# State-space groups: VectorE's two products of decay and scores stand in a row, the fourth modulation tile behind both

## The reference, cut to what matters

```python
mod = (c_act @ w_mod[l] + b_mod[l])[:, None, :]
sh1, sc1, g1, sh2, sc2, g2 = jnp.split(mod, N_MOD, axis=-1)
...
decay = jnp.exp(jnp.where(causal, seg, -jnp.inf))
cb = jnp.einsum('bign,bjgn->bgij', C_c, B_c)
y_intra = jnp.einsum('bgij,bghij,bjghp->bighp', cb, decay, x_c)
y_inter = jnp.einsum('bign,bghpn->bighp', C_c, state) * jnp.exp(cum)[..., None]
```

## Time and profile before

| | us |
|---|---|
| median of three runs | 923.65 |
| the profiled execution | 924.05 |
| its span, first to last instruction | 922.3 |
| TensorE busy | 909.6 (99%) |
| VectorE busy | 703.8 (76%) |
| ScalarE busy | 563.2 (61%) |
| GpSimd busy | 101.4 (11%) |

### The profile page before, as it was taken

One profiled execution on the slowest core, in us unless ns is written; L12 is line 12 of the kernel. 1 busy time (PEld: TensorE's weight loads), 2 busy tenths in 40 slices (PEclk: granted clock), 3 DMA queues, 4 the chain that ended last, 5 costly groups with the idle time before them and its releaser, 6 DMA issues.

```text
span 922.3 us, 17427 instructions
## 1 busy us (share of the span) xinstructions
PE 909.6 (99%) x6694; PEld 845.0 (92%) x6694; DVE 703.8 (76%) x951; ACT 563.2 (61%) x828; POOL 101.4 (11%) x91
## 2 busy tenths in 40 slices
PE   8999999999999999999999999999999999999997
PEld 5799999999999999989888888999879999999886
DVE  5957888888898978568777556689886898777663
ACT  4376655677788775446555345576765776666453
POOL 0000300023423400010000001403100200000001
PEclk9999999999999999999999999999999999999999
DMA  9954565577778756755666656545423366655661
GB/s 352 358 185 157 163 192 181 182 236 239 228 229 259 241 161 204 227 160 172 195 189 193 187 183 186 164 133 182 137 92 124 116 195 189 202 184 181 197 209 49
DMA packets 85596, 175.55 MB, mean 190 GB/s; under 512 B 5440, under 2 KB 46944, under 8 KB 85536
## 3 DMA queue, kind: packets, MB, share of 16 engines
q1 hardware_dynamic: 85024, 173.13, 58.2%
q0 software_dynamic: 368, 1.31, 0.4%
q10 hardware_dynamic: 144, 0.27, 0.1%
HBM read 173.65 MB, written 1.05 MB: 189 GB/s over the span
## 4 chain that ended last, share of the span: by engine, by line
PE 79%; DVE 9%; DMA 4%; ACT 3%; issue 3%; POOL 1%; DVEq 0%; SPq 0%; ACTq 0%; POOLq 0%
PE proj_ps L1717 17%; PE proj_ps L1700 13%; PE proj_ps L1701 13%; PE proj_ps L1702 13%; PE proj_ps L1720 9%; DVE mod_acc L1009 4%; DMA raw<-in_panels 3%; DVE w_lo L997 2%; PE proj_ps L1789 1%; PE proj_ps L1790 1%; PE proj_ps L1791 1%; DMA mod_first<-in_panels 1%; PE aux L2128 1%; PE aux L1821 1%; PE aux L1830 1%
## 5 line engine op out<-in xcount | busy, mean ns | idle before, releaser
L997 DVE TENSOR_TENSOR w_lo<-raw,w_hi 128x1024 fp32r<-128x1024 f32 x276 | 341.7, 1250 | 127.4 <-ACT w_hi L504 126.7
L504 ACT CAST w_hi<-raw 128x1024 fp32r<-128x1024 f32 x276 | 286.2, 1047 | 175.5 <-PE proj_ps L1702 69.6
L1700 PE MATMUL proj_ps<-act_pair,w_hi 128*128 128x256 f32 x1016 | 290.4, 286 | 0.0
L1701 PE MATMUL proj_ps<-act_pair,w_hi 128*128 128x256 f32 x1016 | 287.3, 283 | 0.0
L1702 PE MATMUL proj_ps<-act_pair,w_lo 128*128 128x256 f32 x1016 | 287.3, 283 | 0.0
L1700 PEld LDWEIGHTS proj_ps<-act_pair,w_hi 128*128 128x128 f32 x1016 | 194.7, 192 | 2.6 <-issue 0.8
L1701 PEld LDWEIGHTS proj_ps<-act_pair,w_hi 128*128 128x128 f32 x1016 | 194.7, 192 | 0.8
L1702 PEld LDWEIGHTS proj_ps<-act_pair,w_lo 128*128 128x128 f32 x1016 | 194.7, 192 | 0.0
L1717 PE MATMUL proj_ps<-ff_pair,w_hi 128*128 128x512 f32 x256 | 69.9, 394 | 0.0
L1717 PE MATMUL proj_ps<-act_pair,w_hi 128*128 128x512 f32 x248 | 67.7, 394 | 0.0
L452 POOL TENSOR_TENSOR tmp_b<-tmp_b 128x512 f32<-128x512 f32 x4 | 5.2, 1293 | 453.1 <-ACT tmp_b L527 453.1
(11 more groups left out here) (360 smaller groups left out, 1630.7 us busy)
## 6 DMA issues: line engine op xcount, KB each, us to landing
raw<-in_panels SPq DMA_DIRECT2D x308, 512.0 KB, 3.9
mod_first<-in_panels SPq DMA_DIRECT2D x16, 512.0 KB, 10.4
xres<-in_x_t SPq DMA_DIRECT2D x2, 512.0 KB, 5.6
wst<-in_ws_t POOLq DMA_DIRECT2D x1, 512.0 KB, 4.0
bs_sb<-in_bs_rows POOLq DMA_DIRECT2D x1, 512.0 KB, 4.7
level_sb<-in_levels SPq DMA_DIRECT2D x1, 512.0 KB, 4.7
out_t<-tmp_a SPq DMA_DIRECT2D x1, 512.0 KB, 2.6
out_t<-tmp_a SPq DMA_DIRECT2D x1, 384.0 KB, 3.0
```

The lines of the kernel that those rows point to most:

```text
L504: nc.scalar.copy(w_hi[:, s, :], raw[:, s, :]).then_inc(hi_done, 1)
L997: tt(out=w_lo[:, s, :], in0=raw[:, s, :], in1=w_hi[:, s, :].bitcast(F32), op=ALU.subtract).then_inc(taken, 1)
L1700: mm(dst, hi, xh, start=first and k == 0 and nt % 2 == 0, stop=False, skip_group_check=True)
L1701: mm(dst, hi, xl, start=False, stop=False, skip_group_check=True)
```

## The change

In each group VectorE's modulation tile 3 and the product of chunk 1 change places. Tile 2 stays ahead of the product of chunk 0, though the code names it in another place. No instruction is added or removed.

```diff
                 mod_panel_of(1)
+                mod_panel_of(2)
                 for c in range(2):
-                    mod_panel_of(2 + c)
                     dve.wait_ge(S["decay_ok"], g * 2 + (c + 1))
                     dve.wait_ge(S["cbm_ok"], g + 1)
                     tt(out=decay[:, c], in0=decay[:, c], in1=spread(cbm[:, c], 1, HPG), op=ALU.mult).then_inc(S["m_ok"], 1)
+                mod_panel_of(3)
                 for s in range(2):
                     split_lo(g + (GROUP["zg"] + 2), s)
```

## The result

The changed kernel takes 930.83 us in the median of four runs, the kernel before 923.16 us in four runs beside it: 1.0103 times as long (95% interval 1.0077 to 1.0129), 7.7 us slower. The four runs of the changed kernel took 930.17, 930.46, 931.20 and 938.23 us. The prediction was 929.7, in a range of 925.0 to 933.5. The profiled execution has a span of 929.5 us against 922.3, at a mean clock of 0.999.

The account below looks back on a forecast made before the run. The prediction took a ring of waiting engines through tile 3 and slot 3's transfer as the bound: it grows 7.1 us, 6.0 reach the end, giving 929.65 on the 923.65 median, stated as 929.7, range 925.0 to 933.5.

Parts of the forecast that it names:

- The ring: VectorE's tile 3, slot 3's transfer, ScalarE's rounding, copy and SiLU, VectorE's gate, next group's tile 3: one turn 17.28 us.
- Tile 3 comes later: On VectorE, tile 3 ends 1.18 us later in five of groups 0 to 6, 0.60 in groups 1 and 3: 7.1 us.
- GpSimd beside VectorE: `a_upto_hi`, two tiles in 3.47 us, was read as slowed by about half, not held for a whole instruction.
- ScalarE already waits for slot 3: ScalarE waits 1.80 us for group 2's tile, so a later landing passes on whole; only group 6 has 0.25 us free.
- The sign of 2 us and over at slot 3: In the changed trace, ScalarE's wait for slot 3 would be 2 us and over in every group.
- Shorter transfers and group 6's interference cancel: Slot 3's faster transfers win about 0.8 us, GpSimd's interference in group 6 adds 0.84; the sum stays at 7.1 us.
- What TensorE feels: TensorE's waits at the products move to L1965, for `xdt`; it is 5.3 us late there in group 7, later 6.2.
- 6.0 us reach the end: Of the ring's 7.1 us growth, 6.0 us were taken to reach the kernel's end through TensorE.
- The cover of 1.84 us at group 7: In group 7 `xdt` ends at 315.27 and TensorE's L1965 starts at 317.11, so 1.84 us of delay is hidden.
- Rival C: GpSimd holds VectorE instruction by instruction: tile 3 1.0 us later still in five groups, 935 us in all; chance 0.12.
- Rivals A and B: A: ring has room, three product waits gained, 921.3 us, chance 0.11. B: little ring growth reaches TensorE, 924.8, chance 0.13.

Follow-up runs that it names:

- the opposite order: Kernel before with modulation tiles 1, 2 and 3 of each group ahead of both products: 922.24 us against 922.96, ratio 0.9987.
- the cut: Kernel before, but in groups 0 to 6 ScalarE and VectorE take slot 3's weights from a tensor already there: 921.94 us against 922.97, ratio 0.9987.
- the lighter GpSimd work: GpSimd's two `a_upto_hi` tiles cut to one head of four in groups 0 to 6: order of before 922.42 us, changed order 923.6, against 923.41.
- second trace: The changed kernel run once more, nothing else changed: 930.96 us against 923.41 for the kernel before, ratio 1.008.
- moving that read: Changed kernel with VectorE reading the modulation columns ahead of the gate in odd groups: 931.38 us against 922.97 for the kernel before, ratio 1.0093.
- the cut, changed kernel: Changed kernel with slot 3's weights in groups 0 to 6 taken from a tensor already there, not the transfer: 921.64 us, ratio 0.9992.
- the odd half of the change: Kernel before with the new order in groups 1, 3, 5 and 7 only: 926.93 us against 922.96, ratio 1.0049.

## Why the prediction was right

*The ring bounds the stage, and tile 3 is on it.* Shown for the changed order: with the ring cut it costs -0.3 us, whole it costs 7.7 us. For the order of before the ring was hardly longer than TensorE's own turn, as the opposite order, the cut and the lighter GpSimd work, the last two in the order of before, gained only 0.7 to 1.0 us, none told from no change.

*Tile 3 comes later by 1.18 or 0.60 us a group, 7.1 in all.* The mechanism holds; the size was too small. From `xdt` to tile 3 the seven groups 0 to 6 add up to 49.4 us before, and to 59.4 and 58.3 us in the two traces of the changed kernel: 10.0 and 8.9 us more. The prediction had about 8.2 us a group; groups 1 to 6 have 8.3 to 8.5, group 0 has 9.14 and 7.92. What was wrong is the assumption that tile 3 and the product take the same time in either order, since GpSimd's work beside them is the same.

*GpSimd beside VectorE: "slowed by about half, not held for a whole GpSimd instruction".* This reading was wrong, and it hid the missing part. It took GpSimd's two tiles in 3.47 us for 1.73 us of work each. But such a tile takes 1.03 us where nothing holds it, and in the stage 1.49 or 2.02 us. The first row is from before the stage, the next two from group 2 before, the last two from group 2 of the changed kernel:

```profile
111.20 1.03 POOL L414 TENSOR_TENSOR a_upto_hi<-a_hi,square 128x512 fp32r<-128x512 f32 x1
...
230.82 1.51 DVE L1255 TENSOR_TENSOR decay<-decay,cbm 128x512 f32<-128x512 f32 x1 [0.19 <-DVE mod_acc L1009]
231.74 1.49 POOL L414 TENSOR_TENSOR a_upto_hi<-a_hi,square 128x512 fp32r<-128x512 f32 x1
...
233.46 1.30 POOL L428 TENSOR_TENSOR c_in<-c_in,stg 128x512 f32<-128x512 f32 x1 [2.27 <-ACT c_in L704]
234.71 1.49 POOL L414 TENSOR_TENSOR a_upto_hi<-a_hi,square 128x512 fp32r<-128x512 f32 x1
```

Put in the order of their ends, these instructions alternate, each a fixed time behind the other engine's:

| group 2 before | ends | behind the last | group 2 changed | ends | behind the last |
|---|---|---|---|---|---|
| GpSimd `c_in` | 231.78 | | GpSimd `c_in` | 234.76 | |
| product | 232.33 | 0.55 | product | 235.30 | 0.55 |
| GpSimd tile | 233.23 | 0.90 | GpSimd tile | 236.20 | 0.90 |
| tile 3 | 234.31 | 1.08 | product | 236.75 | 0.55 |
| GpSimd tile | 235.21 | 0.90 | GpSimd tile | 237.65 | 0.90 |
| product | 235.75 | 0.55 | tile 3 | 238.73 | 1.08 |

So each instruction waits for the other engine's whole instruction, and the durations in the rows hold that wait. The change puts a product and also a GpSimd tile ahead of tile 3: 0.55 + 0.90 = 1.45 us, which is what groups 2 and 4 show (8.42 - 6.97 = 1.45), and not 1.18.

*ScalarE already waits for slot 3.* Right: its waits for the stream went up by 9.2 us, 8.3 of them at slot 3, VectorE's at the gate by 4.8. The sign of 2 us and over at slot 3 came in six of the seven groups; in group 2 it is 0.71 us, behind 1.44 us at slot 2.

*Shorter transfers and group 6's interference cancel.* Nearly: the interval from tile 3's end to the next `xdt`, summed over seven turns, is 73.3 us after and 74.7 before, 1.4 us won back (2.1 in the second trace), and group 6 added 2.1 us, 0.9 more than the 1.18. Both terms were there. Not foreseen was that group 1's transfer took longer, 4.44 us in the chain above in place of 3.56.

*What TensorE feels.* Here a step failed, though not the one that sets the total. The waits at the products did go, and the odd groups wait at L1966 for `xdt`, but the even groups 2, 4 and 6 wait at L1962, ahead of it, for the columns that VectorE reads behind the gate. TensorE had hardly any cover there, as a row of the kernel before (PEld is TensorE's loading of weights) already showed:

```profile
PEld aux L1961 <- DVE modc L1033: 0.6, 2, 0.3
```

For the total it did not matter, as moving that read showed; for the split over the groups it did, 3.8 and 4.0 us in place of 5 and 1.

*6.0 us reach the end.* 7.7 us by the medians, 7.2 by the spans. The cover of 1.84 us at group 7 held: `xdt` came 8.8 us later there, and TensorE's L1966 starts at 324.10 in place of 317.11, 7.0 us later. The term was undersized because 7.1 us stood in it for the ring's growth. That 929.7 came so near to 930.83 is in part luck: tile 3's delay was 1.8 to 2.9 us more than the 7.1, and the 1.4 to 2.1 us won back elsewhere took most of that off again.

*Rival C, GpSimd and VectorE exclude each other.* Its mechanism is what the rows show; its price did not come. It gave about 9.2 us from `xdt` to tile 3 in the even groups and a time of 935; measured were 8.4 to 8.5 in groups 2, 4 and 6, and 930.83. The price was too high because it gave each GpSimd tile 1.73 us of its own, where the table above has 0.90 behind VectorE's. For the same reason its argument against itself fails: the first GpSimd tile of group 2 ended at 233.23 and not at 233.47, and tile 3 ended 1.08 us behind it. The rule of the Trainium skill, SBUF — State Buffer, section "SBUF: two separate sides", that the later of the two blocks for the whole instruction, agrees with this case's trace, in group 2 by 0.55, 0.90 and 1.08 us from one end to the next.

*Rivals A and B.* Nothing of the 2.7 us at the products was gained in any run that brought them forward; the small shift in every group is what the lighter GpSimd work gave, and there the loss was 1.2 us.

The cut kernels' spans are 920.6 and 918.8 us, up to 3.5 us below before's 922.3, but their medians only 1.0 to 1.3 us below before's. Most of that is the choice of the profiled execution: before's 924.05 us lie 1.1 us above the median of 922.97, and the 920.50 us of the cut, changed kernel are the shortest of its twelve. Left open is why single executions of one kernel differ by that much and more (921.07 to 928.47 us for the kernel before in 27), and why the odd half of the change costs 4 us where its ring grew by 2.2.

## What to carry to other kernels

An instruction that frees a buffer is a deadline of its own, even on an engine that is idle a quarter of the time: follow what its release starts, through the transfer and the engines behind it, until it comes back or ends. When a wait of the bounding engine is to be removed, ask first whether that engine is late or only shows how late a ring is; here 2.7 us of waits were removed and 8.5 us came, and removing 5.6 us of these again changed nothing. To find out, cut the ring at one link and compare the two orders. And where two engines hold each other up, a duration in a row is work and waiting together: read how far one end lies behind the other engine's end.

## What the runs showed of the hardware

VectorE and GpSimd hold each other up instruction by instruction, in both directions. In both traces, between 188 and 326 us, a product that had to wait for GpSimd's `c_in` or `a_upto_hi` ends 0.55 us behind it, a modulation tile 1.08 us, and a GpSimd tile of `a_upto_hi` ends 0.90 us behind VectorE's product or modulation tile, each to 0.01 us. By themselves they take 0.69 us, 1.27 us (217.84 above) and 1.03 us (111.20 above). Two products in a row take 2.70 or 2.97 us in groups 1 to 3 of the changed kernel, and GpSimd's two tiles took 3.46 to 3.48 us in every group before, where one of them waited for a modulation tile, and 2.93 us in the even groups of the changed kernel, where they waited for products alone:

```profile
234.71 2.93 POOL L414 TENSOR_TENSOR a_upto_hi<-a_hi,square 128x512 fp32r<-128x512 f32 x2
```

The granted clock stayed at 1.00 through TensorE's waits of up to 2.7 us in the changed kernel: the stage between 190 and 345 us, by engine, then clock, DMA share and GB/s.

```profile
190.00:345.00 155.00, 146.44 (x1243) 139.54 (x1242) 130.06 (x130) 118.81 (x204) 45.96 (x40) 1.00 0.69 226
```
